# Attention in two layers: products with the values 64 columns wide, and ScalarE as the copier of the turned probabilities in the second layer

## The reference, cut to what matters

```
def one(xs):                                   # second layer, a row of the grid
    qi, ii, ro = xs
    ki = k[:, ii]
    vi = v[:, ii]
    bias = rpb_f[:, ro[None, :], coff]
    s_loc = jnp.einsum('bqhd,bkhd->bhqk', qi, ki) * scale + bias[None]
    s_loc = jnp.where(col_ok[None, None], s_loc, NEG_INF)
    s_ctx = jnp.einsum('bqhd,bphd->bhqp', qi, ck) * scale
    p_loc, p_ctx = softmax_parts([s_loc, s_ctx])
    return (jnp.einsum('bhqk,bkhd->bqhd', p_loc, vi)
            + jnp.einsum('bhqp,bphd->bqhd', p_ctx, cv))
```

## Time and profile before

| | |
|---|---|
| median of 3 runs | 4721.29 us (4719.97 to 4725.55) |
| the profiled execution | 4717.61 us |
| its span | 4715.8 us |
| TensorE busy in the span | 3943.4 us (84%) |
| granted TensorE clock over the span, mean | 0.906 of full speed |
| first layer's units | from 364 us to 585 us |
| second layer's units | from 2654 us to 2922 us |

### The profile page before, as it was taken

How to read it: one execution, slowest core, us unless ns; L and a number is a source line. 1 busy time by engine, 2 the same in 40 slices (tenths; PEclk the granted TensorE clock), 3 DMA queues, 4 the chain that set the end, 5 groups by cost and what they waited for, 6 DMA issues and landing times. The chain is left out here.

```text
span 4715.8 us, 62439 instructions
## 1 busy us (share of the span) xinstructions
PE 3943.4 (84%) x25842; PEld 3420.0 (73%) x25842; DVE 1757.2 (37%) x3337; ACT 866.7 (18%) x2008; POOL 683.1 (14%) x521
## 2 busy tenths in 40 slices
PE   4979978986769999996999597438886859999995
PEld 3976623444569999995999475338885659999995
DVE  3245541224531211123123454677876441121112
ACT  2113320001100110012111123424443100011001
POOL 2000110111100011002000000036651101001100
PEclk7988979997889999997999798768997979999998
DMA  4226412314547777773421402332223547777774
GB/s 151 89 82 233 148 67 98 137 40 149 201 148 268 261 266 264 268 257 117 116 89 67 108 8 76 102 88 60 73 65 130 190 154 264 268 259 267 266 268 155
DMA packets 353335, 744.94 MB, mean 158 GB/s; under 512 B 87432, under 2 KB 193559, under 8 KB 351976
## 3 DMA queue, kind: packets, MB, share of 16 engines
q1 hardware_dynamic: 333066, 683.15, 40.9%
q0 software_dynamic: 17392, 57.58, 4.5%
q10 hardware_dynamic: 2618, 0.40, 0.1%
HBM read 635.63 MB, written 106.10 MB: 157 GB/s over the span
## 5 line engine op out<-in xcount | busy, mean ns | idle before, releaser
L1826 PE MATMUL moe_b<-moe_xT,ffn_w 128*128 128x144 f32 x8192 | 1022.9, 287 | 0.0
L1826 PEld LDWEIGHTS moe_b<-moe_xT,ffn_w 128*128 128x128 f32 x8192 | 1012.7, 191 | 1.8
L1826 PE MATMUL moe_b<-moe_gu,ffn_w 128*128 128x144 f32 x4096 | 550.7, 288 | 0.0
L1826 PEld LDWEIGHTS moe_b<-moe_gu,ffn_w 128*128 128x128 f32 x4096 | 516.3, 190 | 4.8
L1871 DVE TENSOR_TENSOR moe_gu<-moe_sg,moe_b 128x144 f32<-128x144 f32 x256 | 77.9, 304 | 782.3 <-PE moe_b L1826 782.3
L1851 ACT ACTIVATE moe_yT<-moe_b 128x144 f32<-128x144 f32 x256 | 74.6, 291 | 1074.8 <-PE moe_b L1826 1074.8
L2380 PE MATMUL gdnc_a<-gdnc_T,gdnc_part 128*128 128x128 f32 x864 | 139.3, 318 | 156.7 <-POOL gdnc_part L2537 88.0
L1859 DVE TENSOR_SCALAR moe_xT<-moe_x,keep_coef 128x128 f32<-128x128 f32 (+1 forms) x544 | 154.7, 346 | 252.2 <-PE moe_x L1778 252.1
L2380 PEld LDWEIGHTS gdnc_a<-gdnc_T,gdnc_part 128*128 128x128 f32 x864 | 128.0, 229 | 162.7 <-POOL gdnc_part L2537 149.9
L1747 POOL DMA_INDIRECT scratch_x<-moe_ys,moe_slot x32 | 51.8, 1619 | 1260.7 <-DVE moe_yp L1881 1260.7
L297 PE MATMUL proj_mm<-proj_hT_low,proj_w_high 128*128 128x384 f32 x576 | 193.2, 335 | 0.0
(11 more groups left out here) (413 smaller groups left out, 6401.2 us busy)
## 6 DMA issues: line engine op xcount, KB each, us to landing
ffn_w<-moe_w_gate SPq DMA_DIRECT2D x32, 4096.0 KB, 15.8
ffn_w<-moe_w_up SPq DMA_DIRECT2D x32, 4096.0 KB, 13.9
ffn_w<-moe_w_down SPq DMA_DIRECT2D x32, 4096.0 KB, 15.7
attnrun_m_w<-w_ada SPq DMA_DIRECT2D x40, 1024.0 KB, 9.4
scratch_conv<-proj_zf POOLq DMA_DIRECT2D x24, 512.0 KB, 3.0
scratch_tm<-proj_tm SPq DMA_DIRECT2D x45, 208.0 KB, 1.9
proj_w_raw<-even_w_in SPq DMA_DIRECT2D x24, 384.0 KB, 4.2
scratch_spec<-filt_res SPq DMA_DIRECT2D x36, 256.0 KB, 2.1
```

What stands on the lines that cost most here:

```text
L1826: mm = nc.tensor.matmul(bk[(m * FC + f) % 3][:, 0:SLOTS], w[m][:, k, f * P:(f + 1) * P], src[:, k, :], start=k == 0, stop=k == KD - 1)
```

## The change

Three edits.

1. In `values`, the streamed block is the 64 columns of the unit's own head instead of the 128 of two, and `po` shrinks from 8 x 128 to 8 x 64 columns (one bank). Both layers.
2. `take_outputs` scales `po` in one VectorE instruction of 512 columns instead of two of 256. Both layers.
3. In the second layer only, `take_probs` moves from VectorE to ScalarE. There it stands behind the exponential of the next unit; `take_turned`, which stood behind the exponential of unit 8k+3, now stands behind that of 8k+2 and the copy of 8k+1.

```
-        po = s.ps("po", [P, 8, P])
+        po = s.ps("po", [P, 8, HD])
...
-            at = P * plan.kv_chunk(h)
-            tiles = [tok[:, k, v_at + at:v_at + at + P] for k in keys]
+            at = P * plan.kv_chunk(h) + HD * plan.chunk_half(h)[1]
+            tiles = [tok[:, k, v_at + at:v_at + at + HD] for k in keys]
...
-                for half in range(2):
...
-                    ins = nc.vector.tensor_tensor(dst, src, r.unsqueeze(2).broadcast_to([P, 4, HD]), ALU.mult)
-                ins.then_inc(o_done, 1)
+                nc.vector.tensor_tensor(o_sb[:, g % 2], po[:], rinv[:, g % 2, :].unsqueeze(2).broadcast_to([P, 8, HD]), ALU.mult).then_inc(o_done, 1)
...
-                if 1 <= u <= NU:
+                if even and 1 <= u <= NU:
                     take_probs(u - 1)
...
+            def take_probs(u):
+                n = plan.columns(units[u][0])
+                if u >= 2:
+                    act.wait_ge(pv_done, u - 1)
+                act.wait_ge(p_turned, u + 1)
+                nc.scalar.activation(pT[:, u % 2, 0:n], slot(("p", u))[:, 0:n], ACT.Copy).then_inc(pT_done, 1)
...
-                if u % 8 == 3 and u >= 8:
+                if not even and u >= 1:
+                    take_probs(u - 1)
+                if u % 8 == (3 if even else 2) and u >= 8:
                     take_turned(u // 8 - 1)
...
+            if not even:
+                take_probs(NU - 1)
```

More of the change, by code:

```diff
@@ L845, in values @@
             t, keys, cached = groups[g]
-            at = P * plan.kv_chunk(h)
-            tiles = [tok[:, k, v_at + at:v_at + at + P] for k in keys]
+            at = P * plan.kv_chunk(h) + HD * plan.chunk_half(h)[1]
+            tiles = [tok[:, k, v_at + at:v_at + at + HD] for k in keys]
             if cached:
-                tiles = [cv[:, at:at + P]] + tiles if even else tiles + [cv[:, at:at + P]]
+                tiles = [cv[:, at:at + HD]] + tiles if even else tiles + [cv[:, at:at + HD]]
             if h == 0 and g >= 1:
```

## The result

The change made the kernel slower: 4892.8 us median of 4 runs (4889.1 to 4895.1) against 4720.6 (4719.9 to 4725.6), ratio 1.036, 95% interval 1.034 to 1.038. I had forecast 4705 us, with 4696 to 4718 as range. The profiled execution took 4894.0 us, 176.4 more than that of before.

A forecast was written before the change was run, and what follows sets the result against it. TensorE was taken as the bound. Unit ends -7.3, gaps -3.5 and clock -5.1 us sum to -15.9 us; against the median of 4721.3 us this gave a forecast of 4705 us, range 4696 to 4718.

The forecast's parts named there:

- What bounds the kernel: Both attention layers: TensorE is the bound, busy 217.6 of 226 and 249.4 of 268 us; everything outside stays.
- Edit 1, the pace: Products of `values`: the load sets the pace, so 64 columns leave them 0.111 us apart, no gain.
- the streamed columns are the price: Rival: `values` takes half its time with 64 columns, -65.7 us and the rest, about 4646 us; chance 0.07.
- Edit 1, 0.054 us at a unit's end: Last product of a unit's `values`: the next stream begins 0.054 us sooner, in 136 units, -7.3 us.
- Edit 2: One VectorE instruction per group in `take_outputs`: can't cost more, lies beside TensorE's work except at gaps, counted 0.
- Edit 3 in the steady part: Second layer's steady units: ScalarE's copy takes 0.85 us, ends 1.65 us before it is needed, cost 0.
- Edit 3 at the gaps and its clock: Second layer's group ends: 0.5 us less per gap at seven gaps, -3.5 us, and fewer clock falls, -5.1 us.
- The clock: Falls to about 0.50 after gaps lose 8.5 us; one long one expected in place of three, -5.1 us, least certain.
- The prediction's own sign of being wrong: Among the signs of being wrong: a mean clock below 0.92 in the second stretch or 0.94 in the first.
- Slower: Rival: 64-column streams idle the array, the clock falls mid-work, once per group in both layers, 54 us, 4756 us; chance 0.06.
- The evidence I put against it: Against the slower rival: first layer's clock stays up through all narrow work, mean 0.94 including the half-speed start.
- The first layer: Listed as a sign of being right: the first layer shorter by about 4 us.

## Why the prediction was wrong

**What bounds the kernel: right.** TensorE is the bound in each of these kernels, and nothing outside the two layers moved, except through the clock.

**Edit 1, the pace: right.** At full clock in the first layer the loads of `values` stay 0.111 us apart with 64 columns beside them: six of them span 0.75 us, (0.75 - 0.19)/5 = 0.112. The rival "the streamed columns are the price" has fallen. The Trainium skill's "TensorE: Matmul & The Clock Gate" gives the gap by streamed columns, under "Back-to-back issue gap", for an isolated product; the same section says that in a stream of loads and products both set the spacing. This trace agrees with the second: 0.112 us with 64 columns, as with 128.

**Edit 1, 0.054 us at a unit's end: right in size.** 2.54 against 2.59 us with four tiles, 3.09 against 3.14 with five, 3.64 against 3.69 with six. 96 columns give 0.03, half of it.

**Edit 2: right, worth little.** One instruction of 0.69 us where two took 0.76, hidden except at a group's end.

**Edit 3 in the steady part: right.** The copy of 768 columns takes 0.81 us (I had 0.85), and no steady turning waits for it.

**Edit 3 at the gaps and its clock: right together.** With 128 columns it shortened the second layer from 264.2 to 254.3 us. I had -3.5 and -5.1 us, -8.6 in sum; it was -9.9. The waits at the group ends gave 4.7 us (13.9 to 9.2), and the falls inside the layer shrank from 17.0 to 3.4 us, at half speed 6.8 us less lost.

**The step that failed is "The clock".** It took edit 3's shorter gaps as all that touches the clock, and wrote -5.1 us for the whole change. It asked how often a fall would come at a group end, at its old length of 3.4 or 6.8 us. It did not ask how the clock comes back, nor how the second layer leaves the 0.50 it starts with. In these runs both hung on what the 128-column streams gave: columns that nobody reads, but work for the array. The rows of before showed that there was something to ask: the layer was at 0.51 until 2670, and each fall ended. Against the kernel with edit 3 alone, 64 columns in the second layer were worth +170.2 + 9.9 = +180 us, where the term had a gain. The prediction's own sign of being wrong came: a mean clock of 0.50 in the second stretch and 0.92 in the first.

**The rival "Slower" named the right condition and the wrong event.** 64-column streams do leave the array idle in `values`, but the clock did not fall in the middle of the work; in the kernels that held it, steady narrow units hold it too. What narrow units did not do was keep it over a group's pause, or get it back, but for the one rise after 112 us without pauses. So its price, sixteen falls of 3.4 us or 54 us, was a third of what one loss without an end took. The evidence I put against it, "in the first layer the clock stays up through all the narrow work", was true and still is at 64 columns. It does not carry over: that layer has next to no pauses at its group ends, 0.5 us in 84. I looked at how narrow the streams were and not at what stands between them.

**The first layer: about -4 us expected, little left.** From first scores to last values it went from 218.5 to 217.7 us, and with wide last groups to 216.2. The clock fell at 576 instead of 584 among the one-tile units and rose at 651 instead of 639 in the filters, so the filters' products with their taps start at 702.9 instead of 697.6. With this go the 5 us by which the second layer starts late. The early fall comes with the narrow one-tile units: it came between 574 and 579 us in all eleven kernels that have them, and between 581 and 589 in the eight profiled executions with 128 columns there. The late rise goes with it only in part: it came near 650 in seven of the eleven and near 637 in the other four, and at 653 in one of the eight. So those 5 us are not shown to be the change's own.

## What to carry to other kernels

Streamed columns that nobody reads can be what keeps TensorE at 2.4 GHz: before cutting them, see at which clock the stretch starts, what TensorE did when it rose, and how long its waits are. If narrow streams are wanted, first remove the pauses (here with the PSUM bank that they set free) and raise the clock once with dense products inside a wait that is there anyway: together, with wide values in the first layer's last two groups, 4697.5 us, where the changed kernel took 4892.8. Nearly half of what this version gains over the kernel before (0.26 of 0.57%) needs no narrow stream: the copy on ScalarE alone gave 4710.1.

## What the runs showed of the hardware that I had not expected

- TensorE can be busy without a gap for 40 us at a stretch and stay at 1.2 GHz: 425.4 of 436 us busy, clock 0.50. The Trainium skill ("TensorE: Matmul & The Clock Gate", section "Why this matters for your kernels") advises continuous busy time against the low clock. This trace doesn't agree that this is enough.
- Pauses of at most 1.3 us at the group ends mostly leave the clock at 1.00 when 128 columns stand around them: 60 of 63 group ends passed without a fall, and the three falls ended after 3.4 to 10.2 us. With 64 columns (one narrow unit behind a wide group was enough) the first such pause brought 0.50 for the rest of the layer, 370 us, in two kernels with one execution each.
- Narrow units at 0.50 mostly stayed there. Of the six kernels in which they stood at 0.50 with nothing wide or extra behind (the changed one, the ones with the copies on VectorE, with products ahead of the scores, with the wide first group, with the products but the shared bank, and with the bank alone), one left it, after 112 us, and that was the one without pauses.
